# First feed-forward: weight quarters in the order dense, dense, modulation, modulation

## Chip, cores and metric

The kernel runs on one core of one Trainium2 chip. The metric is the device time of one execution in microseconds (us), the median of the runs made.

## What is computed

One inference step of a two-layer encoder over 384 token rows: 256 of a prompt (one stream) and 16 for each of 8 running streams. Width is 2048, feed-forward width 5632. Each layer has a token mixer (layer 0 attention, layer 1 causal pooling) and a SwiGLU feed-forward, and each of these four sub-layers is modulated by vectors that depend on the stream alone:

```
mod = silu(c) @ w_ada + b_ada              # nine streams, 2048 x 12288 weights in each layer
h   = rms_norm(x, g_ffn) * (1 + scale2) + shift2
x   = x + gate2 * ((silu(h @ w_gate) * (h @ w_up)) @ w_down)
```

Everything is float32. Weights are read from HBM once.

## The kernel before, in words

**Units.** Weights come in units of 1 MB: 512 rows by 512 columns, as 4 row tiles of 128 rows. There are four slots for units. `raw[:, s]` is the buffer that a DMA fills, and `w_hi`/`w_lo` share their bytes with `w_top`/`w_mid`. Unit `n` of weight group `W` is in slot `n % 4` (`unit`, "quarter" in the change's name).

**Dense units** (`w_gate`, `w_up`, `w_down`). ScalarE copies `raw` to the rounded `w_hi` (L569), and VectorE computes `w_lo = raw - w_hi` (L956). TensorE then takes three matmuls for each pair of tiles (`product`: L1511, L1512, L1513), 128x128 weights against 384 tokens, 48 matmuls a unit.

**Modulation units** (`w_ada`). ScalarE copies `raw` to bf16 `w_top` (L576), and VectorE makes two more bf16 pieces in two instructions (`mid`, L961 and L963). TensorE takes 12 bf16 matmuls of 512 columns (`ada_sub`, L1538), each with a stationary operand only 32 columns wide, so that four of them stand side by side in the array (`q = C32 * (i % 4)`). Four modulation units make one block of 512 modulation values. ScalarE then copies the block out (`mod_out`, L596), TensorE transposes it (`ada_turn`, four matmuls at L1547), and VectorE sums it into `modT` (`mod_in`, L986 and L989).

**One chunk of the first feed-forward** (`mixed_chunk`, 11 chunks in a hardware loop on TensorE, of which the first 10 are a loop on ScalarE and VectorE). A chunk is 512 of the 5632 hidden features and takes 20 units: 0 to 7 the gate's four dense units in turn with the four modulation units of block `a`, 8 to 15 the same for up and block `a + 1`, and 16 to 19 the four dense units of the down product. The gate accumulates in banks 4 to 7, up in banks 0 to 3. Block `a` accumulates in bank 3, block `a + 1` in bank 7.

**What sets the order.** Each engine's order is written out by hand and engines meet through counting semaphores. SP loads the units in their order, a slot's next unit as soon as VectorE has read `raw` (`load` waits for `lo_ready`). ScalarE converts unit `n + 4` only once TensorE has used unit `n` (`free` waits for `sub_used`). VectorE follows ScalarE (`hi_ready`), and TensorE waits for `lo_ready` at a dense unit and for `top_rest` at a modulation unit. Between weights, ScalarE applies Silu to the gate (`gate_out`, L851) and rounds the product (`acts_hi`, L846), VectorE multiplies gate by up (`times_up`, L1378) and adds the down product into the residual `x` (`down_add`, L1065, L1072, L1075), and GpSimd makes `act_lo` (L539).

**Before the first chunk** the residual is normalised (`norm_apply(1, W_FFN0)`). VectorE scales four groups of feature tiles (`norm_scale`, L1030 and following), ScalarE shifts and rounds them into `h_hi` (L643, L647), and VectorE writes `h_lo` (`norm_split`, L1042). Units 2 and 3 of the first chunk are converted in between (`BETWEEN`), 0 and 1 earlier, in the last block of the attention's output product. TensorE starts unit 0 when the first half of group 0 is there, and needs group `j` for the gate's `j`-th dense unit.

Of the kernel before, what the change touches and what calls it, by code (L numbers as in the profile page):

```python
# [25 lines left out]
ds = bass.ds  # L26
# [26 lines left out]
W_FFN0 = W_O + 8  # L53
# [48 lines left out]
def encoder_step(nc, x_prompt, x_sample, c_prompt, c_sample, cache_k, cache_v, state_pool,  # L102
# [5 lines left out]
    with ctx:  # L108
# [24 lines left out]
        h_hi, H0 = nxt("h_hi", [P, KT, TOK], f32r)  # L133
# [115 lines left out]
        def rows(w):  # L249

            return w.rearrange("(k p) n -> p k n", p=P)
# [35 lines left out]
        def unit(W, n):  # L287

            return W + n // 4, n % 4

        def y_bank(q):
            return down_bank(q)

# [33 lines left out]
        def _(sp):  # L327
            def load(W, s, src):
                sp.wait_ge(lo_ready, 4 * W + s - 3)
                sp.dma_start(raw[:, s], src).then_inc(raw_loaded[s], 16)  # L330
# [26 lines left out]
            def load_pair(W, j, dense, layer, a):  # L357

                for n, src in ((2 * j, dense), (2 * j + 1, ada_src(layer, a, j))):
                    load(*unit(W, n), src)  # L360

            def qkv_rows(n, j):

# [82 lines left out]
            def load_mixed(W, c, layer, a):  # L446

                for i, w in enumerate((w_gate, w_up)):
                    for j in range(4):
                        load_pair(W + 2 * i, j, rows(w[0, j * 512:(j + 1) * 512, ds(c * 512, 512)]), layer, a + i)  # L450
                load_down(W + 4, 0, c)

            load_mixed(W_FFN0, 0, 0, ADA_FFN)
# [101 lines left out]
        def _(act):  # L555
# [21 lines left out]

            def mixed(W, n):

                W, s = unit(W, n)  # L580
                if n % 2:
                    top(W, [s])
                else:
                    hi(W, [s])

            def dense(W, n):

                W, s = unit(W, n)
                hi(W, [s])

            def mod_out(used, a, acc_bank, done=sub_used):

                act.wait_ge(done, used)
                if not isinstance(a, int) or a:
                    act.wait_ge(ada_t, a)
                act.activation(mod[:], bank[:, acc_bank, :], ACT.Copy).then_inc(mod_ready, 1)  # L596
# [251 lines left out]
            def gate_out(used):  # L848

                act.wait_ge(sub_used, used)  # L850
                act.activation(act_f[:], bank[:, 4:8, 0:TOK], ACT.Silu).then_inc(gate_taken, 1)  # L851

            def mixed_chunk(W, c, a, following, last=False):

                for n in range(4, 10):
                    mixed(W, n)
                gate_out(4 * W + 7)
                mixed(W, 10); mod_out(4 * W + 8, a, 3); mixed(W, 11)
                for n in range(12, 16):
                    mixed(W, n)  # L860
                dense(W, 16); dense(W, 17)
                for m in range(4):
                    acts_hi(c, m)
                mod_out(4 * W + 16, a + 1, 7)
                dense(W, 18); dense(W, 19)
                for s in range(4):
                    following(W, 20 + s)
                    if last and s < 3:
                        square(2, s)
                    elif last:  # L870
                        square_last(2)
# [75 lines left out]
        def _(dve):  # L947
# [16 lines left out]

            def mixed(W, n):

                W, s = unit(W, n)
                if n % 2:
                    mid(W, s)
                else:  # L970
                    lo(W, [s])

            def dense(W, n):

                W, s = unit(W, n)
                lo(W, [s])
# [68 lines left out]
            def norm_apply(n, W):  # L1045

                norm_scale(n, 0, 2, 1)
                norm_scale(n, 2, 2, 2)
                norm_split(n, 0, 2, 1, half_ready)
                norm_split(n, 2, 2, 2)  # L1050
                for g in range(1, 4):
                    if g >= 2:
                        dve.wait_ge(h_ready, HR[n] + g - 1)
                    norm_scale(n, 4 * g, 4, g + 2)
                    for s in BETWEEN[n][g]:
                        (mixed if n == 1 else dense)(W, s)
                    if g >= 2:
                        norm_split(n, 4 * g - 4, 4, g + 1)
                norm_split(n, 12, 4, 5)

# [309 lines left out]
            def times_up(c, used):  # L1370

                dve.wait_ge(gate_taken, c + 1)
                for m in range(4):
                    if m < 3:
                        dve.wait_ge(up_tile, 3 * c + m + 1)
                    else:
                        dve.wait_ge(sub_used, used)
                    dve.tensor_tensor(act_f[:, m], act_f[:, m], bank[:, m, 0:TOK], ALU.mult).then_inc(act_f_ready, 1)  # L1378
# [7 lines left out]
            def mixed_chunk(W, c, a, layer, r, following, last=False):  # L1386

                for n in range(4, 12):
                    mixed(W, n)
                mod_in(a, 4)  # L1390
                for n in range(12, 16):
                    mixed(W, n)
                dense(W, 16); dense(W, 17)
                times_up(c, 4 * W + 15)
                dense(W, 18)
                mod_in(a + 1, 3)
                dense(W, 19)
                dve.wait_ge(ada_done, a + 2)
                for s in range(4):
                    down_add(4 * W + 17 + s, s, r, layer, last and s == 3)  # L1400
                    if not last or s < 3:
                        following(W, 20 + s)
                    if last and s < 3:
                        square_sum(2, s)
# [103 lines left out]
        def _(pe):  # L1508
# [18 lines left out]
            def ada_sub(W, n, a, j, acc_bank):  # L1527

                W, s = unit(W, n)
                if j == 0:  # L1530
                    pe.wait_ge(mod_ready, a)
                pe.wait_ge(top_rest, 4 * (a - ADA_QKV) + j + 1)
                for k in range(4):
                    kt = 4 * j + k
                    for piece, w in enumerate((w_top[:, s, 0, k], mid_top(s)[:, k], w_top[:, s, 1, k])):
                        i = 3 * kt + piece
                        q = C32 * (i % 4)
                        last = pe.matmul(bank[q:q + C32, acc_bank, :], c32[:, kt], w, start=(i < 4), stop=(i >= 3 * KT - 4))  # L1538
                last.then_inc(sub_used, 1)

            def ada_turn(a, t_bank):

# [304 lines left out]
            def mixed_chunk(W, c, a, r, hr):  # L1847

                pe.wait_ge(residual_taken, r - 1)
                for j in range(4):  # L1850
                    if j:
                        pe.wait_ge(h_ready, hr + j + 1)
                    else:
                        pe.wait_ge(half_ready, 1)
                    to_features(W, 2 * j, 4, h_hi, h_lo, 4 * j, j == 0, j == 3, second_half=None if j else hr + 1)
                    if j == 0:
                        pe.wait_ge(residual_taken, r)
                    ada_sub(W, 2 * j + 1, a, j, 3)
                for m in range(4):
                    if m == 3:  # L1860
                        pe.wait_ge(mod_ready, a + 1)
                    last = tile_features(W, 8, m, 0, h_hi, h_lo, 0, True, False)
                last.then_inc(sub_used, 1)
                pe.wait_ge(gate_taken, c + 1)
                ada_turn(a, 4)
                ada_sub(W, 9, a + 1, 0, 7)
                for j in (1, 2):
                    to_features(W, 8 + 2 * j, 0, h_hi, h_lo, 4 * j, False, False)
                    ada_sub(W, 9 + 2 * j, a + 1, j, 7)
                up_tail(W, 14)  # L1870
                ada_sub(W, 15, a + 1, 3, 7)

                w, s = unit(W, 16)
                pe.wait_ge(lo_ready, 4 * w + s + 1)
                pe.wait_ge(ada_done, a + 1)
                for k in range(4):
                    pe.wait_ge(act_ready, 4 * c + k + 1)
                    for m in range(3):
                        cols = slice(m * P, (m + 1) * P)
                        product(bank[:, 4 + m, 0:TOK], w_hi[:, s, k, cols], w_lo[:, s, k, cols],  # L1880
                                act_hi[:, k, :], act_lo[:, k, :], k == 0, k == 3)
                ada_turn(a + 1, 3)
                last = tile_features(W, 16, 3, 4, act_hi, act_lo, 0, True, True)
                last.then_inc(sub_used, 1)
                pe.wait_ge(ada_done, a + 2)
                down_rest(W, 16, r)
# [104 lines left out]
```

## Time and profile before

| | |
|---|---|
| median of 3 runs | 3416.63 us |
| lowest and highest | 3412.81 and 3418.68 us |
| span of the profiled execution, first to last instruction | 3414.0 us |
| mean granted TensorE clock (1 is 2.4 GHz) | 0.985 |
| TensorE matmul busy | 3265.0 us, 96% |
| VectorE busy | 2119.0 us, 62% |
| ScalarE busy | 1309.1 us, 38% |
| GpSimd busy | 137.6 us, 4% |
| DMA | 646.49 MB, mean 189 GB/s |

The profiled execution is given by its span; a time of its own outside the span is not listed. Its span is 2.6 us under the median of the runs. Busy time alone doesn't say what an engine's work costs: TensorE's matmuls overlap, each row lasting longer than the distance to the next, so distances between starts are what counts. A timeline line reads: start in us, duration in us, engine, line of the kernel, operation, output and inputs, count, and in brackets how long the engine had been idle and what released it.

### The profile page before, as it was taken

The numbers are of one execution on the slowest core, as the hardware profiler recorded it, in microseconds if no ns is written. First come the engines' busy times: TensorE is split into PE (matmuls) and PEld (weight loads), VectorE is DVE, ScalarE is ACT, GpSimd is POOL, SyncE is SP. The second block draws the span as 40 slices with busy tenths as digits, with TensorE's granted clock in tenths as the row PEclk, the third lists the DMA queues.
The fourth block names the chain that finished last, engine by engine and source line by source line (L and its number), as shares of the span: only waits on it lengthen the run. The fifth ranks groups of instructions, "written<-read, shape, count | busy, mean of one in ns | idle before, by whom it ended". The sixth has DMA issues, their size and how long they took to land.

```text
span 3414.0 us, 47966 instructions
## 1 busy us (share of the span) xinstructions
PE 3265.0 (96%) x20219; PEld 2953.3 (87%) x20219; DVE 2119.0 (62%) x1855; ACT 1309.1 (38%) x994; POOL 137.6 (4%) x124
## 2 busy tenths in 40 slices
PE   7999998889989999999999999769999999999999
PEld 3677776667979999999999999659999999999999
DVE  4488885567887777777776777784344443344443
ACT  3344444455453343334433443443223222322221
POOL 0000000000000000000000000110000000000000
PEclk9999999999999999999999999889999999999999
DMA  9777777877645555556555565544343333333331
GB/s 352 269 263 248 249 244 251 304 278 263 231 160 185 199 206 185 193 176 210 205 177 192 184 209 197 190 158 145 123 131 127 123 124 133 125 123 124 127 130 62
DMA packets 325816, 646.49 MB, mean 189 GB/s; under 512 B 10881, under 2 KB 13513, under 8 KB 325321
## 3 DMA queue, kind: packets, MB, share of 16 engines
q1 hardware_dynamic: 317144, 630.17, 54.1%
q10 hardware_dynamic: 8586, 15.09, 1.3%
q8 instruction: 65, 1.06, 0.1%
q14 instruction: 21, 0.17, 0.0%
HBM read 631.46 MB, written 14.74 MB: 189 GB/s over the span
## 4 chain that ended last, share of the span: by engine, by line
PE 88%; DVE 5%; DMA 4%; ACT 2%; issue 1%; POOL 0%; SPq 0%; ACTq 0%; DVEq 0%; POOLq 0%
PE bank L1511 23%; PE bank L1513 23%; PE bank L1512 23%; PE bank L1595 3%; PE bank L1538 3%; PE bank L1597 3%; PE bank L1596 3%; DMA raw<-in_w_ada 2%; PE bank L1701 1%; DMA raw<-in_cache_v 1%; PE bank L1523 1%; PE bank L1742 1%; DVE w_lo L956 0%; PE bank L1547 0%; DMA early_raw<-in_w_qkv 0%
## 5 line engine op out<-in xcount | busy, mean ns | idle before, releaser
L956 DVE TENSOR_TENSOR w_lo<-raw,w_hi 128x2048 fp32r<-128x2048 f32 x323 | 738.9, 2290 | 877.7 <-ACT w_hi L569 877.7
L569 ACT ACTIVATE w_hi<-raw 128x2048 fp32r<-128x2048 f32 x323 | 616.3, 1915 | 1352.4 <-PE bank L1513 1168.7
L1511 PE MATMUL bank<-h_hi,w_hi 128*128 128x384 f32 x3136 | 1063.9, 339 | 34.3 <-DVE h_lo L1042 24.1
L1512 PE MATMUL bank<-h_lo,w_hi 128*128 128x384 f32 x3136 | 1052.2, 336 | 0.0
L1513 PE MATMUL bank<-h_hi,w_lo 128*128 128x384 f32 x3120 | 1047.7, 336 | 0.0
L1511 PEld LDWEIGHTS bank<-h_hi,w_hi 128*128 128x128 f32 x3136 | 591.9, 189 | 79.3 <-issue 67.1
L1512 PEld LDWEIGHTS bank<-h_lo,w_hi 128*128 128x128 f32 x3136 | 592.3, 189 | 0.0
L1513 PEld LDWEIGHTS bank<-h_hi,w_lo 128*128 128x128 f32 x3120 | 589.0, 189 | 0.0
L1511 PE MATMUL bank<-act_hi,w_hi 128*128 128x384 f32 x1408 | 472.9, 336 | 0.0
L1513 PE MATMUL bank<-act_hi,w_lo 128*128 128x384 f32 x1408 | 470.6, 334 | 0.0
L1512 PE MATMUL bank<-act_lo,w_hi 128*128 128x384 f32 x1408 | 470.5, 334 | 0.0
L961 DVE TENSOR_TENSOR w_mid<-raw,w_top 128x2048 f32<-128x2048 f32 x144 | 329.1, 2285 | 14.7 <-ACT w_top L576 14.7
L576 ACT ACTIVATE w_top<-raw 128x2048 bf16<-128x2048 f32 x144 | 273.7, 1901 | 161.7 <-PE bank L1513 128.5
L963 DVE TENSOR_TENSOR w_top<-w_mid 128x2048 bf16<-128x2048 f32 x144 | 330.0, 2292 | 5.0
L1511 PEld LDWEIGHTS bank<-act_hi,w_hi 128*128 128x128 f32 x1408 | 264.3, 188 | 4.8 <-POOL act_lo L539 4.8
L1512 PEld LDWEIGHTS bank<-act_lo,w_hi 128*128 128x128 f32 x1408 | 264.4, 188 | 0.0
L1513 PEld LDWEIGHTS bank<-act_hi,w_lo 128*128 128x128 f32 x1408 | 264.3, 188 | 0.0
L1595 PE MATMUL bank<-w_hi,h_hi 128*128 128x512 f32 x480 | 192.4, 401 | 2.6 <-DVE w_lo L956 2.6
L539 POOL TENSOR_TENSOR act_lo<-act_f,act_hi 128x384 fp32r<-128x384 f32 x88 | 87.9, 1015 | 2652.0 <-ACT act_hi L846 2650.7
L1597 PE MATMUL bank<-w_hi,h_lo 128*128 128x512 f32 x480 | 187.7, 391 | 0.0
L1596 PE MATMUL bank<-w_lo,h_hi 128*128 128x512 f32 x480 | 187.4, 390 | 0.0
L1072 DVE SCALAR_TENSOR_TENSOR x<-bank,modT,x 128x256 f32<-128x256 f32 x384 | 158.6, 475 | 0.0
(231 smaller groups left out, 2501.5 us busy)
## 6 DMA issues: line engine op xcount, KB each, us to landing
raw<-in_w_ada SPq DMA_DIRECT2D x192, 1024.0 KB, 5.8
raw<-in_w_gate SPq DMA_DIRECT2D x88, 1024.0 KB, 5.2
raw<-in_w_up SPq DMA_DIRECT2D x88, 1024.0 KB, 5.2
raw<-in_w_down SPq DMA_DIRECT2D x88, 1024.0 KB, 5.1
raw<-in_w_qkv SPq DMA_DIRECT2D x40, 1024.0 KB, 5.2
raw<-in_cache_k SPq DMA_DIRECT2D x32, 1024.0 KB, 6.0
raw<-in_cache_v SPq DMA_DIRECT2D x32, 1024.0 KB, 7.2
raw<-in_w_o SPq DMA_DIRECT2D x15, 1024.0 KB, 5.1
```

Source lines behind the costliest of these rows:

```text
L569: act.activation(w_hi[:, s], raw[:, s], ACT.Copy).then_inc(hi_ready, 1)
L576: act.activation(w_top[:, s, 0], raw[:, s], ACT.Copy).then_inc(hi_ready, 1)
L956: dve.tensor_tensor(w_lo[:, s], raw[:, s], w_hi[:, s].bitcast(f32), ALU.subtract).then_inc(lo_ready, 1)
L961: dve.tensor_tensor(w_mid[:, s], raw[:, s], w_top[:, s, 0], ALU.subtract).then_inc(lo_ready, 1)
L963: dve.tensor_tensor(w_top[:, s, 1], w_mid[:, s], mid_top(s), ALU.subtract).then_inc(top_rest, 1)
L1072: step.mark(dve.scalar_tensor_tensor(xv, ps[:, k, 0:PROMPT], mod[:, k, 0:1], xv, ALU.mult, ALU.add))
L1511: pe.matmul(out, w, a, start=start, stop=False)
L1512: pe.matmul(out, w, al, start=False, stop=False)
L1513: return pe.matmul(out, wl, a, start=False, stop=stop)
L1595: pe.matmul(out, h_hi[:, kt, cols], w_hi[:, s, k], start=(kt == 0), stop=False)
L1596: pe.matmul(out, h_hi[:, kt, cols], w_lo[:, s, k], start=False, stop=False)
L1597: last = pe.matmul(out, h_lo[:, kt, cols], w_hi[:, s, k], start=False, stop=(kt == KT - 1))
```

## The change

In the first feed-forward alone, the units of each group of four go dense, dense, modulation, modulation (before: dense, modulation, dense, modulation). SP loads them in that order (`load_four`), and ScalarE and VectorE choose the conversion by `in_ffn`. TensorE takes two dense units and then the two modulation units behind one another (`ada_two`). ScalarE's Silu moves with the gate's end, from behind unit 6 to behind unit 5. The second down unit (17) now takes the slot of the last up unit (13), so ScalarE converts it behind `acts_hi`, and VectorE multiplies gate by up ahead of the split of unit 17. In the normalisation ahead of the first chunk VectorE writes `h_lo` of group `g - 1` ahead of converting the weight unit.

```diff
+        def in_ffn(W, n):
+            return not isinstance(W, int) or W + n // 4 >= W_FFN0
...
+            def load_four(W, f, dense, layer, a):
+
+                for i in range(2):
+                    load(*unit(W, 4 * f + i), dense(2 * f + i))
+                for i in range(2):
+                    load(*unit(W, 4 * f + 2 + i), ada_src(layer, a, 2 * f + i))
...
-                    for j in range(4):
-                        load_pair(W + 2 * i, j, rows(w[0, j * 512:(j + 1) * 512, ds(c * 512, 512)]), layer, a + i)
+                    for f in range(2):
+                        load_four(W + 2 * i, f, lambda j: rows(w[0, j * 512:(j + 1) * 512, ds(c * 512, 512)]), layer, a + i)
...
             def mixed(W, n):
+                rest = n % 4 >= 2 if in_ffn(W, n) else n % 2
                 W, s = unit(W, n)
-                if n % 2:
+                if rest:
...
             def mixed_chunk(...):
-                for n in range(4, 10):
+                for n in range(4, 9):
                     mixed(W, n)
-                gate_out(4 * W + 7)
-                mixed(W, 10); mod_out(4 * W + 8, a, 3); mixed(W, 11)
+                gate_out(4 * W + 6)
+                mixed(W, 9); mod_out(4 * W + 8, a, 3); mixed(W, 10); mixed(W, 11)
                 for n in range(12, 16):
                     mixed(W, n)
-                dense(W, 16); dense(W, 17)
+                dense(W, 16)
                 for m in range(4):
                     acts_hi(c, m)
                 mod_out(4 * W + 16, a + 1, 7)
-                dense(W, 18); dense(W, 19)
+                dense(W, 17); dense(W, 18); dense(W, 19)
...
                     norm_scale(n, 4 * g, 4, g + 2)
+                    if n == 1 and g >= 2:
+                        norm_split(n, 4 * g - 4, 4, g + 1)
                     for s in BETWEEN[n][g]:
                         (mixed if n == 1 else dense)(W, s)
-                    if g >= 2:
+                    if n != 1 and g >= 2:
                         norm_split(n, 4 * g - 4, 4, g + 1)
...
-                dense(W, 16); dense(W, 17)
-                times_up(c, 4 * W + 15)
-                dense(W, 18)
+                dense(W, 16)
+                times_up(c, 4 * W + 14)
+                dense(W, 17); dense(W, 18)
...
+            def ada_two(W, f, a, acc_bank):
+
+                for i in range(2):
+                    ada_sub(W, 4 * f + 2 + i, a, 2 * f + i, acc_bank)
...
-                    to_features(W, 2 * j, 4, h_hi, h_lo, 4 * j, j == 0, j == 3, second_half=None if j else hr + 1)
-                    if j == 0:
+                    to_features(W, j + j // 2 * 2, 4, h_hi, h_lo, 4 * j, j == 0, j == 3, second_half=None if j else hr + 1)
+                    if j == 1:
                         pe.wait_ge(residual_taken, r)
-                    ada_sub(W, 2 * j + 1, a, j, 3)
+                    if j % 2:
+                        ada_two(W, j // 2, a, 3)
...
-                ada_sub(W, 9, a + 1, 0, 7)
-                for j in (1, 2):
-                    to_features(W, 8 + 2 * j, 0, h_hi, h_lo, 4 * j, False, False)
-                    ada_sub(W, 9 + 2 * j, a + 1, j, 7)
-                up_tail(W, 14)
-                ada_sub(W, 15, a + 1, 3, 7)
+                to_features(W, 9, 0, h_hi, h_lo, 4, False, False)
+                ada_two(W + 2, 0, a + 1, 7)
+                to_features(W, 12, 0, h_hi, h_lo, 8, False, False)
+                up_tail(W, 13)
+                ada_two(W + 2, 1, a + 1, 7)
```

## Rows read from the trace of the kernel before

**Rows 1.** The page: the chain that ended last, by engine.

```profile
PE 88%; DVE 5%; DMA 4%; ACT 2%; issue 1%; POOL 0%; SPq 0%; ACTq 0%; DVEq 0%; POOLq 0%
```

**Rows 2.** Stretches: two whole chunks; us, engines' busy us (count), PEclk, DMA share, GB/s.

```profile
1014.20:1123.03 108.83, 108.83 (x684) 102.48 (x688) 78.34 (x60) 44.15 (x29) 3.97 (x4) 1.00 0.57 195
...
1340.66:1449.47 108.81, 108.81 (x684) 102.46 (x684) 78.34 (x60) 44.15 (x29) 3.97 (x4) 1.00 0.57 193
```

**Rows 3.** Timeline, ScalarE: Silu; conversions started by TensorE freeing a slot.

```profile
1340.66 1.45 ACT L851 ACTIVATE act_f<-bank 128x1536 f32<-128x1536 f32 x1 [4.31 <-PE bank L1513]
...
1388.21 1.92 ACT L569 ACTIVATE w_hi<-raw 128x2048 fp32r<-128x2048 f32 x1 [4.59 <-PE bank L1513]
1396.53 1.91 ACT L576 ACTIVATE w_top<-raw 128x2048 bf16<-128x2048 f32 x1 [6.40 <-PE bank L1513]
...
1421.49 1.91 ACT L569 ACTIVATE w_hi<-raw 128x2048 fp32r<-128x2048 f32 x1 [5.05 <-PE bank L1513]
...
1430.82 1.91 ACT L569 ACTIVATE w_hi<-raw 128x2048 fp32r<-128x2048 f32 x1 [5.61 <-PE bank L1513]
```

**Rows 4.** Timeline, TensorE: one modulation unit between two dense ones.

```profile
1340.28 0.34 PE L1513 MATMUL bank<-h_hi,w_lo 128*128 128x384 f32 x1
1340.55 0.39 PE L1538 MATMUL bank<-w_top,c 128*32 128x512 bf16 x1
...
1340.78 0.39 PE L1538 MATMUL bank<-w_mid,c 128*32 128x512 bf16 x1
...
1341.00 0.41 PE L1538 MATMUL bank<-w_mid,c 128*32 128x512 bf16 x1
...
1341.62 0.33 PE L1512 MATMUL bank<-h_lo,w_hi 128*128 128x384 f32 x1
```

**Rows 5.** Timeline, TensorE: transposes of a modulation block inside a dense unit.

```profile
1385.28 0.34 PE L1513 MATMUL bank<-act_hi,w_lo 128*128 128x384 f32 x1
1385.46 0.60 PE L1547 MATMUL bank<-ident,mod 128*128 128x128 f32 x4
...
1386.07 0.34 PE L1512 MATMUL bank<-act_lo,w_hi 128*128 128x384 f32 x1
```

**Rows 6.** Timeline, TensorE in the attention: a long run of 32-column matmuls.

```profile
784.75 2.69 PE L1742 MATMUL bank<-raw,zs_past 128*32 128x128 f32 x92
```

**Rows 7.** Timeline, VectorE behind the Silu: units 10 and 11, then unit 12.

```profile
1343.95 2.29 DVE L956 TENSOR_TENSOR w_lo<-raw,w_hi 128x2048 fp32r<-128x2048 f32 x1 [3.85 <-ACT w_hi L569]
1346.23 2.29 DVE L961 TENSOR_TENSOR w_mid<-raw,w_top 128x2048 f32<-128x2048 f32 x1
1348.56 2.29 DVE L963 TENSOR_TENSOR w_top<-w_mid 128x2048 bf16<-128x2048 f32 x1
1350.76 0.60 DVE L986 TENSOR_REDUCE modT<-bank 128x432 f32 x1
...
1351.93 2.29 DVE L956 TENSOR_TENSOR w_lo<-raw,w_hi 128x2048 fp32r<-128x2048 f32 x1 [0.23 <-ACT w_hi L569]
```

**Rows 8.** The page: DMA issues, KB each, us from issue to landing.

```profile
raw<-in_w_ada SPq DMA_DIRECT2D x192, 1024.0 KB, 5.8
```

**Rows 9.** Timeline, VectorE around the first chunk: units 2, 3, `h_lo` of group 1, unit 4.

```profile
973.60 2.29 DVE L956 TENSOR_TENSOR w_lo<-raw,w_hi 128x2048 fp32r<-128x2048 f32 x1
...
978.92 2.28 DVE L961 TENSOR_TENSOR w_mid<-raw,w_top 128x2048 f32<-128x2048 f32 x1
...
983.45 1.75 DVE L1042 TENSOR_TENSOR h_lo<-nbuf,h_hi 128x1536 fp32r<-128x1536 f32 x1
...
993.89 2.29 DVE L956 TENSOR_TENSOR w_lo<-raw,w_hi 128x2048 fp32r<-128x2048 f32 x1 [1.47 <-ACT w_hi L569]
```

**Rows 10.** Timeline, TensorE in the first chunk: starts of units 2 and 4.

```profile
985.33 0.55 PE L1511 MATMUL bank<-h_hi,w_hi 128*128 128x384 f32 x1 [3.80 <-DVE h_lo L1042]
...
996.23 0.44 PE L1511 MATMUL bank<-h_hi,w_hi 128*128 128x384 f32 x1
```

**Rows 11.** Stretch, TensorE, unit 2 of the first chunk: us, busy us (count), PEclk, DMA share, GB/s.

```profile
985.33:995.40 10.07, 10.07 (x48) 0.83 0.03 11
```

More of the change, by code:

```diff
@@ L965, in mixed @@
             def mixed(W, n):
+                rest = n % 4 >= 2 if in_ffn(W, n) else n % 2
                 W, s = unit(W, n)
-                if n % 2:
+                if rest:
                     mid(W, s)
```

## The prediction

> **What bounds the kernel now.** I read the page's chain first: TensorE holds 88% of it [rows 1]. Then one chunk of the first feed-forward, cut from Silu to Silu: 108.8 us, in which TensorE is busy from end to end at the full clock (2.4 GHz), VectorE for 78.3 and ScalarE for 44.2 [rows 2]. So in this stage nothing but TensorE's own spacing counts, and the other engines and the DMAs only have to stay in time. Last the timelines, for that spacing. ScalarE's conversions there start when TensorE frees a slot, so the distance of two of them is what TensorE took for what lies between: 8.32 us for one dense unit of the down product, 9.33 for a dense unit and a modulation unit [rows 3]. A modulation unit thus costs 1.01 us. Its 12 matmuls account for less: they go four at a time, and the three waves start 0.225 apart, which is 0.675 in all [rows 4]. The rest is at the two changes of form. From the last dense matmul to the first wave it is 0.27 where dense matmuls are 8.32/48 = 0.173 apart, and from the last wave to the second dense matmul it is 0.62 where 0.225 + 0.173 would do. That is 0.10 and 0.22, together 0.32; as 1.01 - 0.675 it comes to 0.33 [rows 3, 4]. **A pair of changes of form costs 0.33 us**, and a chunk has eight pairs.
>
> A check: 12 dense units at 8.32, 8 modulation units at 1.01 and two transposes. A set of transposes takes 1386.07 - 1385.46 - 0.173 = 0.44 inside a dense unit [rows 5]. The sum is 99.8 + 8.1 + 0.9 = 108.8, which is the chunk [rows 2].
>
> **The change, part by part.** *The order of units on TensorE.* Each chunk then has four runs of two modulation units where it had eight of one. Matmuls, loads and bytes are the same, and four pairs of changes go: 4 x 0.33 = 1.3 us a chunk. No row shows two modulation units in a row, so I bound a merge. At the least it gives nothing, if the second unit starts as expensively as after a dense one; a loss is excluded, since no change of form is added. At the most it gives 0.33, since the columns still have to pass. I take 0.33, because of the nearest row: 92 matmuls with the same 32-column form follow one another in 2.69 us, 27 to 29 ns each, across the waits and counts between groups of 16 [rows 6]. Nothing is paid there at a boundary, and the pace is twice the 0.225/4 = 56 ns wanted here.
>
> The first of the two transposes now sits between two dense units, not ahead of a modulation unit. I cost that at nothing: the second sits between dense matmuls already, and the sum above closes with the same 0.44 for both.
>
> *What must stay in time in a chunk.* VectorE has the tight spot behind the Silu, where unit 9's split is followed by four instructions for units 10 and 11 back to back, by the sums of the block (`mod_in`), and only then by unit 12's split. Measured from the Silu's start: unit 9's split starts at 3.3, as unit 10's does now, and two modulation splits take 4 instructions of 2.2 to 2.3, to 14.6. The sums take 1351.93 - 1350.76 = 1.2 with a short idle time in it, and the split of unit 12 takes 2.2, so it is there at 18.0 [rows 7]. TensorE then wants unit 12 after two modulation units, unit 8, a set of transposes, unit 9 and two more modulation units: 2 x (2 x 0.675 + 0.33) + 2 x 8.32 + 0.44 = 20.4. **Slack 2.4 us.** Unit 10 itself is wanted at 18.7 and there at 10.1; unit 11 is there at 14.6. A unit's raw slot is refilled 5.8 us after its issue [rows 8], and the load of unit 12 is issued when unit 8's split ends, ahead of the Silu. The queue of SP meets the same 20 loads and waits as before, and what stands behind a waiting load is a unit wanted later.
>
> *Gate times up ahead of unit 17's split.* Unit 17 now uses the slot of unit 13, which ends the up product. From that end, E, TensorE takes two modulation units and unit 16 with its transposes: 1.7 + 8.3 + 0.4 = 10.4. ScalarE waits for the two (1.7), copies the block out (not rowed; allowed as long as a conversion, 1.9), converts 17 (1.9) and VectorE splits it (2.3): E + 7.8 at the latest [rows 3, 7]. Slack 2.6 us, so nothing is paid. Were the split left ahead, ScalarE and VectorE would wait for each other, since `acts_hi` now stands ahead of unit 17. The multiplication itself gains nothing: unit 16 was waiting for neither. The activations even get 0.675 more, since two modulation units now stand between up's end and unit 16. The Silu moves with the gate's end, and bank 3 is copied out ahead of unit 8's fourth tile, 6 us on. The adds into `x` keep their places between the down units; bank 3 is wanted one dense unit later than before.
>
> *The first chunk pays.* Unit 2 becomes a modulation unit, so VectorE has two instructions for it where it had one: 983.45 - 978.92 = 4.53 against 2.29, so 2.2 to 2.3 more, between 973.60 and unit 4's split at 993.89 [rows 9]. TensorE starts unit 4 when that split is done (993.89 + 2.29 = 996.18, start 996.23) [rows 9, 10]. Everything between is one chain, VectorE's norm of group 3, ScalarE's rounding and conversion of unit 4, so unit 4 starts **2.3 us later**, near 998.5. The new place of `norm_split` helps what isn't last: unit 1's features come at 973.60 + 4.53 + 3.1 + 1.8 = 983.0, against 985.3 for unit 2 before (3.1 is what lies between 973.60 + 2.2 and 978.92) [rows 9, 10]. Unit 1 and two modulation units are over by 983.1 + 10.1 + 1.7 = 994.9 at the latest, so TensorE then stands idle for at least 3.6 us ahead of unit 4. Before, a gap of 3.8 stood ahead of unit 2, and that unit ran at a mean clock of 0.83, starting at the lower level (1.2 GHz): 10.07 us, not 8.32 [rows 10, 11]. I expect the same for unit 4, **1.7 us more**. Bounds: 0, if the clock holds, and 3.4, if the lower level lasts twice as long as in that unit. The first of this chunk's merges falls ahead of unit 4's wait and gives nothing; three are left. The last attention block has one VectorE instruction less (unit 1 is dense now), ahead of a wait for TensorE: nothing.
>
> *The last chunk* converts pool weights behind its down units as before, and the rest of the kernel starts earlier by the sum.
>
> **The sum.** Ten chunks with 4 merges and one with 3: 43 x 0.33 = 14.2 us less. First chunk 2.3 + 1.7 = 4.0 us more. Together 10.2 less: 3414.0 to 3403.8 for the span, and from the median, which stands 2.6 above the span, 3416.6 to **3406.4 us**, 0.30% less. About 0.2% (6.8 us) is what a measurement of this kernel tells from no change.
>
> **Rivals.** *(A) Merges give little.* A run of 24 small matmuls outlasts what TensorE's queue has read ahead during a dense unit, and from there goes at the pace of issue. Within a unit all 12 keep 56 ns [rows 4], which a short head start could cover; against it speak the 92 matmuls at under 30 ns [rows 6]. At no gain at all the first chunk's 4.0 stays: 3420.6. At half: 3416.6 + 4.0 - 7.1 = 3413.5. Both count as no change. The Trainium skill, in "TensorE: Matmul & The Clock Gate", section "Wait — 56ns, not 53.3ns?", has a rule on this side: where decoding in hardware is off, the sequencer needs about 62 ns for each matmul, and that binds when the array's work is shorter. By it a second unit would take 12 x 62 = 0.74 us, and and 43 merges would give an estimated 43 x 0.26 = 11.2 us, 3409.4; the row of 92 disagrees with it.
>
> *(B) VectorE falls behind unit 12: slower.* Two modulation splits behind one another leave 2.4 us. If the queue from unit 9 to unit 12 comes late by more than that, through a late load or slower instructions, TensorE stands in each of 10 or 11 chunks. It decides from 2.4 + 1.3 = 3.7 us late in each chunk, where the gain is gone. At 5 late it costs 2.6 x 11 = 29 against 10.2 gained: 3435. Against it: the chunks repeat to 0.02 us [rows 2], and VectorE's instructions to 0.1 [rows 7].
>
> *(C) The first chunk costs more*, as unit 4's wait pushes units 5 to 7 too. Their splits follow 2 to 3 us behind each other and have 8 us each, so I give it 2 us at most: 3408.4. It is part of the forecast's range.
>
> **How the numbers follow.** Forecast with (C) 0.78, its range 3402 to 3411: the merge 0.30 to 0.36 (1.3 us each way), the clock 0 to 3.4 (1.7 each way), (C) +2, and runs that differ by a few us. (A) 0.16, (B) 0.06. The limit for faster is 3409.8, and of the forecast's 0.78 some 0.08 lies above it. Faster 0.70, same 0.24 (0.16 + 0.08), slower 0.06. The range is 3401 to 3414: the forecast's, one more us below for the runs, and (A) down to half of the gain.
>
> **What would show it.** Right: chunks of 107.5 us from Silu to Silu, with TensorE busy throughout; in a merged run six waves 0.225 apart and one gap of 0.27 ahead; unit 12's split some 2.4 ahead of its matmuls; unit 4 of the first chunk starting near 998.5 and running at a mean clock near 0.83. Wrong: a gap between the third and fourth waves or a pace over 0.225 (A), TensorE waiting for L956 at unit 12 or 17 (B), or a first chunk over 4 us later at its second Silu than units and merges make it (C).

## The result and the profile after

The changed kernel takes 3403.8 us (median of 5 runs, 3402.8 to 3406.0); the kernel before 3414.8 (median of 5: the three runs above and two more). The ratio is 0.9965, 95% interval 0.9953 to 0.9977: faster by 0.35%, a small effect whose interval leaves out 1. In later runs, again with the kernel before beside it, the ratio was 0.9965 once more (0.9954 to 0.9977). The forecast was 3406.4, between 3401 and 3414.

The profiled execution has a span of 3401.1 us. Two whole chunks, cut from Silu to Silu, in the stretches of the changed kernel (engines' busy us and counts, PEclk, DMA share, GB/s):

```profile
1014.59:1122.07 107.48, 107.48 (x684) 102.98 (x684) 78.13 (x60) 44.29 (x29) 3.93 (x4) 1.00 0.57 191
1337.03:1444.51 107.48, 107.48 (x684) 102.98 (x684) 78.11 (x60) 44.28 (x29) 3.92 (x4) 1.00 0.58 195
```

A chunk lasts 107.48 us where it lasted 108.81 to 108.83 [rows 2], with the same 684 matmuls, TensorE still busy from end to end and the other engines' work unchanged. That is 1.33 less, ten times from the first Silu to the eleventh. Where it comes from is seen in the timeline of TensorE, at the two modulation units behind the gate of the first chunk:

```profile
1014.22 0.34 PE L1527 MATMUL bank<-h_hi,w_lo 128*128 128x384 f32 x1
1014.48 0.39 PE L1552 MATMUL bank<-w_top,c 128*32 128x512 bf16 x1
...
1014.71 0.39 PE L1552 MATMUL bank<-w_mid,c 128*32 128x512 bf16 x1
...
1014.93 0.41 PE L1552 MATMUL bank<-w_mid,c 128*32 128x512 bf16 x1
...
1015.16 0.39 PE L1552 MATMUL bank<-w_mid,c 128*32 128x512 bf16 x1
...
1015.37 0.41 PE L1552 MATMUL bank<-w_mid,c 128*32 128x512 bf16 x2
...
1015.61 0.40 PE L1552 MATMUL bank<-w_mid,c 128*32 128x512 bf16 x1
...
1016.21 0.33 PE L1526 MATMUL bank<-h_lo,w_hi 128*128 128x384 f32 x1
```

Six waves (four matmuls each), 0.21 to 0.24 apart, and nothing between the third and the fourth, where the second unit begins. The gap ahead (0.26) and the slow return behind (0.60 from the last wave to the second dense matmul) are those of a single unit [rows 4], and are paid once for two.

The first chunk has grown. TensorE's timeline there, with the starts of units 0, 1 and 4, and ahead of them the start of unit 0 in the kernel before:

```profile
969.54 0.68 PE L1511 MATMUL bank<-h_hi,w_hi 128*128 128x384 f32 x1 [8.56 <-DVE h_lo L1042]
```

```profile
966.99 0.68 PE L1525 MATMUL bank<-h_hi,w_hi 128*128 128x384 f32 x1 [8.56 <-DVE h_lo L1054]
980.59 0.44 PE L1525 MATMUL bank<-h_hi,w_hi 128*128 128x384 f32 x1 [2.54 <-DVE h_lo L1054]
...
995.88 0.69 PE L1525 MATMUL bank<-h_hi,w_hi 128*128 128x384 f32 x1 [5.25 <-DVE w_lo L967]
```

And the stretches of unit 1 (all engines, as above) and of unit 4 (TensorE alone: busy us, count, PEclk, DMA share, GB/s):

```profile
980.59:989.00 8.41, 8.41 (x48) 8.27 (x48) 8.31 (x6) 2.65 (x6) 0.00 (x0) 1.00 0.39 125
```

```profile
995.88:1006.00 10.12, 10.12 (x48) 0.81 0.89 308
```

Unit 4 starts 28.9 us after unit 0, where it was 26.7 (996.23 [rows 10] less 969.54). It was released by its own split, and it runs at a mean clock of 0.81, starting at 1.2 GHz. Unit 1, behind a gap of 2.5 us, ran at the full clock.

Single executions differ ahead of all this. Unit 0 started at 967.0 here and at 969.5 before, and between 967 and 977 in the runs below, in stages that the change leaves as they were but for one VectorE instruction less in the last attention block. So the trace is compared from unit 0's start on, to the first Silu of the second feed-forward (before, then after):

```profile
2336.07 1.46 ACT L851 ACTIVATE act_f<-bank 128x1536 f32<-128x1536 f32 x1 [5.10 <-PE bank L1513]
```

```profile
2323.14 1.46 ACT L862 ACTIVATE act_f<-bank 128x1536 f32<-128x1536 f32 x1 [5.10 <-PE bank L1527]
```

That is 1366.5 us before (2336.07 - 969.54) and 1356.2 after (2323.14 - 966.99): **10.4 us less**, where the sum said 10.2. It is made of 13.3 less between the first and the eleventh Silu and 2.9 more ahead of the first; behind the eleventh Silu the two take 233.7 and 233.8.

### The profile page after: what moved, and what is told of

It is laid out like the page before. It is cut to its first block, busy times and chain, and to the rows that moved or that the text cites. A ratio compares the mean times of both kernels' runs of the same rounds, so it can differ in the third digit from the quotient of the medians.

```text
span 3401.1 us, 47966 instructions
## 1 busy us (share of the span) xinstructions
PE 3250.1 (96%) x20219; PEld 2957.6 (87%) x20219; DVE 2116.7 (62%) x1855; ACT 1310.5 (39%) x994; POOL 137.1 (4%) x124
## 4 chain that ended last, share of the span: by engine, by line
PE 87%; DVE 5%; DMA 4%; ACT 2%; issue 1%; POOL 0%; SPq 0%; ACTq 0%; DVEq 0%; POOLq 0%
PE bank L1525 23%; PE bank L1527 23%; PE bank L1526 23%; PE bank L1614 3%; PE bank L1616 3%; PE bank L1615 3%; PE bank L1552 3%; DMA raw<-in_w_ada 3%; PE bank L1720 1%; DMA raw<-in_cache_v 1%; PE bank L1537 1%; DMA raw<-in_cache_k 0%; DVE w_lo L967 0%; PE bank L1566 0%; DMA early_raw<-in_w_qkv 0%
```

## The experiments

Theory: TensorE bounds the stage, each merge of two modulation units saves one pair of changes of form, 0.33 us, and the first chunk pays some 4 us because VectorE is late for unit 4 and the clock has fallen by then. Rivals: the gain comes from another part of the change; the second modulation unit is slowed by issue; VectorE's queue has less room than worked out. Ratios are to the kernel before on the same chip. "First Silu" is its start after the start of unit 0, which is 44.7 before (1014.22 - 969.54) and 47.6 after (1014.59 - 966.99).

**The new order in the up half alone.** The gate half, its loads, the Silu's place and the norm are as before.

```diff
-                rest = n % 4 >= 2 if in_ffn(W, n) else n % 2
+                rest = n % 4 >= 2 if in_ffn(W, n) and 8 <= n < 16 and not (isinstance(W, int) and W < W_FFN0) else n % 2
...
-                    to_features(W, j + j // 2 * 2, 4, h_hi, h_lo, 4 * j, j == 0, j == 3, second_half=None if j else hr + 1)
-                    if j == 1:
+                    to_features(W, 2 * j, 4, h_hi, h_lo, 4 * j, j == 0, j == 3, second_half=None if j else hr + 1)
+                    if j == 0:
                         pe.wait_ge(residual_taken, r)
-                    if j % 2:
-                        ada_two(W, j // 2, a, 3)
+                    ada_sub(W, 2 * j + 1, a, j, 3)
```

> The new order in the up half alone (units 8 to 15); the gate half keeps dense, modulation, dense, modulation, and the norm ahead of the first chunk keeps its old order. If each merge of two modulation units is worth 0.33 us and nothing else counts, a chunk lasts 108.81 - 2 x 0.33 = 108.15 us from Silu to Silu, the first chunk is as in the kernel before (first Silu 44.7 us after unit 0's start), and 22 merges give 7.3 us: ratio 0.998. If the gain comes from elsewhere (the Silu's new place, the slots of the down units), the chunk is not halfway but at 107.5 or at 108.8.

Ratio 0.9982 (0.9972 to 0.9991). First Silu at 44.65. The stretch of its first whole chunk:

```profile
1015.80:1123.95 108.15, 108.15 (x684) 102.68 (x684) 78.13 (x60) 44.28 (x29) 3.93 (x4) 1.00 0.59 196
```

108.15, halfway to the hundredth: the gain goes with the number of merges. The Silu's place and the gate's slots, which are the old ones here, have no share in it; neither has unit 17's new place, which is in this kernel and adds nothing to the two merges.

**The first chunk's gate half in the old order**, all else changed. The first chunk is taken out of the loops of TensorE, ScalarE and VectorE.

```diff
-            return not isinstance(W, int) or W + n // 4 >= W_FFN0
+            return not isinstance(W, int) or W + n // 4 >= W_FFN0 + 2
...
+            mixed_chunk(W_FFN0, 0, ADA_FFN, R_FFN0, 4, first=True)
-            with pe.Fori(0, CHUNKS) as c:
+            with pe.Fori(1, CHUNKS) as c:
...
+                    if first:
+                        ada_sub(W, 2 * j + 1, a, j, 3)
+                    elif j % 2:
+                        ada_two(W, j // 2, a, 3)
```

> The changed kernel, with the first chunk's gate half and the norm in the old order. If the first chunk pays what the trace says (unit 8 stands 3.6 us later after unit 0's start than before, 49.3 against 45.7), that comes back: first Silu 44.7 us after unit 0's start, chunks of 107.48, and 3.6 us less than the changed kernel: ratio to the kernel before 0.996. If the first chunk's cost is only moved elsewhere, the total stays that of the changed kernel (0.9965).

Ratio 0.9962 (0.9947 to 0.9977), median 3401.2. First Silu at 45.5 (1022.22 - 976.76), 0.8 later than expected, with unit 2 at a mean clock of 0.76 instead of 0.83 [rows 11]. Chunks of 107.44. From unit 0 to the first Silu of the second feed-forward: 1354.5 (2331.23 - 976.76), 1.7 less than the changed kernel, not 3.6. Of the missing 1.9 us, 0.8 is the first Silu. The rest lies behind the eleventh Silu, where this execution took 235.2 to the next feed-forward (2331.23 - 2095.99) and the changed kernel's 233.8. Why that stretch varies stays open; it was 230.6 to 235.2 in all kernels here but the one with unit 17 split ahead. Up to the eleventh Silu 3.2 of the 3.6 us do come back (1119.2 from unit 0's start against 1122.4). The total can't tell it.

**`norm_split` back behind the weight unit** in the norm ahead of the first chunk.

```diff
-                    if n == 1 and g >= 2:
-                        norm_split(n, 4 * g - 4, 4, g + 1)
                     for s in BETWEEN[n][g]:
                         (mixed if n == 1 else dense)(W, s)
-                    if n != 1 and g >= 2:
+                    if g >= 2:
                         norm_split(n, 4 * g - 4, 4, g + 1)
```

> The changed kernel with the write of h_lo of the group before put back behind the conversion of the weight unit. Theory (the clock decides): unit 1 starts 4.5 us later, 18.1 after unit 0's start, after a long gap and so at the lower clock, and ends at 28.1; with two modulation units unit 4 starts at 29.8 instead of 28.9, but without a gap and so at the full clock: the first Silu comes 46.7 after unit 0's start, 0.9 us earlier than in the changed kernel (47.6). Rival (the move was needed): unit 4 is late and at the lower clock too, first Silu at 48.4.

First Silu at 46.8 (1014.80 - 968.03), against 46.7 expected. A single run, 3403.1 us. The stretch of unit 1, then that of unit 4 (TensorE alone):

```profile
986.16:996.20 10.04, 10.04 (x48) 0.81 0.02 9
...
998.00:1006.50 8.50, 8.50 (x50) 1.00 0.92 308
```

Unit 1 is 4.5 us later, behind a gap of 7.35, and is the one that runs at the lower clock. Unit 4 then follows without a gap, at the full clock. The move of `norm_split` that the change brought makes unit 1 early and TensorE idle later on, and costs 0.8 us net. One execution shows it; five with the move (and no matmuls of no use) had their first Silu at 47.4 to 48.6, all later than here.

**Unit 17 split ahead of gate times up**, as before the change, on both engines.

```diff
-                dense(W, 16)
+                dense(W, 16); dense(W, 17)
                 for m in range(4):
                     acts_hi(c, m)
                 mod_out(4 * W + 16, a + 1, 7)
-                dense(W, 17); dense(W, 18); dense(W, 19)
+                dense(W, 18); dense(W, 19)
...
-                dense(W, 16)
+                dense(W, 16); dense(W, 17)
                 times_up(c, 4 * W + 14)
-                dense(W, 17); dense(W, 18)
+                dense(W, 18)
```

> The changed kernel with unit 17 converted and split ahead of gate times up again, on ScalarE and on VectorE. From the end E of up's last unit: conversion of 17 to E + 1.9, its split to E + 4.2, four products of 0.5, rounding and GpSimd 1.6 behind the first: the first activation tile is there at E + 6.3, where TensorE wants it at E + 1.7. Theory (the second part of the change is needed): TensorE stands 4.6 us in each chunk, so 112.1 us from Silu to Silu, and up to 1.7 more if the clock falls; in all 51 to 70 us over the changed kernel. Rival (it is hidden): 107.5.

A single run, 3481.0 us. Stretches of two chunks, and what TensorE's weight load (PEld) waited for in the second (us in all, times, longest):

```profile
1131.06:1246.20 115.14, 110.16 (x684) 105.59 (x684) 78.23 (x60) 44.20 (x29) 3.89 (x4) 0.97 0.55 182
1246.20:1360.21 114.01, 109.03 (x684) 104.46 (x684) 78.24 (x60) 44.20 (x29) 3.90 (x4) 0.99 0.56 184
```

```profile
PEld bank L1525 <- POOL act_lo L549: 5.5, 1, 5.5
```

TensorE stands 4.98 us in each chunk (115.14 - 110.16), for the first of the four `act_lo` tiles that GpSimd makes, where 4.6 was expected. It is also busy 1.5 to 2.7 us longer for the same matmuls, at a mean clock of 0.97 to 0.99: the clock falls behind the gap. The mean of nine chunks is 114.4 us ((2046.49 - 1016.61) / 9), 7.0 over the changed kernel's. In all it is 77 us over the changed kernel (3481.0 - 3403.8), more than the 51 to 70 expected, since both the gap and the clock cost more than allowed for. So the second part of the change is what the first part needs: without it the kernel is 65 us slower than the kernel before beside it (3415.8).

**One, then two more instructions on VectorE** ahead of units 10, 11 and 12 in each chunk.

```diff
                 for n in range(4, 12):
+                    if n == 9:
+                        w, s = unit(W, n)
+                        dve.wait_ge(hi_ready, 4 * w + s + 1)
+                        for _ in range(1):
+                            step.mark(dve.tensor_tensor(w_lo[:, s], raw[:, s], w_hi[:, s].bitcast(f32), ALU.subtract))
+                            own()
                     mixed(W, n)
```

> The changed kernel with one more VectorE instruction of 2.2 us in each chunk (the split of unit 9 is written twice), ahead of units 10, 11 and 12. In the changed kernel unit 12's split ends 17.8 us after the Silu's start and TensorE wants it at 20.4, by the sums of the rows: slack 2.5. One more instruction must cost nothing: 107.5 us from Silu to Silu. If the slack is less than the rows say, the chunk is longer by the missing part.

107.48 us from Silu to Silu (1123.14 to 1230.62), 3404.6 us in a single run. In the changed kernel unit 12's split is VectorE's:

```profile
1352.54 2.29 DVE L967 TENSOR_TENSOR w_lo<-raw,w_hi 128x2048 fp32r<-128x2048 f32 x1
```

It starts 15.5 behind the Silu at 1337.03 and ends at 17.8. Here it starts at 17.7 (1355.85 - 1338.11). It costs nothing in a chunk.

> The same with two more instructions, 4.5 us: 2.0 over the slack, so 109.5 us from Silu to Silu and TensorE waiting for w_lo at unit 12, some 22 us in all. If VectorE's queue had more room than worked out, 107.5.

With `range(2)`: 3439.2 us in a single run. Six of ten chunks take 109.77 us, where 109.5 was expected, but four take 111.3. From unit 0 to the second feed-forward it is 29.8 us more than in the changed kernel (1386.0 against 1356.2), where some 22 was expected. Two chunks, then a stretch of 4 us inside the first of them, right behind its gap; and a wait of this kind in another chunk (us in all, times, longest):

```profile
1132.30:1243.60 111.30, 109.23 (x684) 0.98 0.56 188
1353.40:1463.17 109.77, 107.70 (x684) 1.00 0.57 191
...
1154.00:1158.00 4.00, 3.29 (x14) 0.76 0.43 132
```

```profile
PE bank L1531 <- DVE w_lo L967: 2.1, 1, 2.1
```

Both chunks have the same gap of 2.07 us (111.30 - 109.23, 109.77 - 107.70), so the slack was 4.5 - 2.1 = 2.4 us. In the first the clock fell behind it and took 1.5 us more.

**Matmuls of no use in the first chunk's gap.** TensorE's first chunk stands outside the loop; the results go to a bank that the up product overwrites.

```diff
                         ada_two(W, j // 2, a, 3)
+                    if first and j == 1:
+                        for i in range(26):
+                            pe.matmul(bank[:, 1, 0:TOK], h_hi[:, i % 8, 0:P], h_hi[:, i % 8, :], start=True, stop=True)
```

> The changed kernel with 26 matmuls of no use (the result is overwritten) behind the first two modulation units of the first chunk, some 4.5 us, in the gap of 5.3 us that stands ahead of unit 4. If the lower clock in unit 4 comes from that gap, unit 4 runs at the full clock and the first Silu comes 45.9 us after unit 0's start, 1.7 less than 47.6. If something else slows unit 4 (its operands, the engines beside it), it stays at 47.6.

First Silu at 46.7 (1020.20 - 973.50), 0.8 later than expected. The stretches of unit 1 and unit 4:

```profile
987.17:997.20 10.03, 10.03 (x48) 0.83 0.33 105
1003.30:1011.70 8.40, 8.40 (x51) 1.00 0.96 337
```

Unit 4 did run at the full clock, beside the same engines and on the same operands: the gap is the cause. But in this execution the lower clock fell into unit 1, behind a gap of 3.2, so the matmuls of no use began 1.6 later than planned for, and the last of them pushed unit 4 back from 28.9 to 29.8.

**Another order of VectorE's norm**, alone:

```diff
+                    norm_scale(n, 4, 4, 3)
+                    dve.wait_ge(h_ready, HR[n] + 1)
+                    norm_scale(n, 8, 4, 4)
+                    norm_split(n, 4, 4, 3)
+                    mixed(W, 2)
+                    dve.wait_ge(h_ready, HR[n] + 2)
+                    norm_scale(n, 12, 4, 5)
+                    mixed(W, 3)
+                    norm_split(n, 8, 4, 4)
+                    norm_split(n, 12, 4, 5)
```

> The changed kernel with VectorE's work ahead of the first chunk in another order: norm of groups 1 and 2, h_lo of group 1, unit 2, norm of group 3, unit 3, h_lo of groups 2 and 3, unit 4. If VectorE's row of instructions sets unit 4's start, with idle time in it that the order can take out, unit 4 starts 26.9 us after unit 0, not 28.9, still at the lower clock: first Silu at 45.6. If ScalarE or a DMA sets it, it stays near 47.6.

TensorE's timeline: unit 0, the first matmul of a modulation unit that had to wait (unit 3), unit 4.

```profile
972.07 0.68 PE L1537 MATMUL bank<-h_hi,w_hi 128*128 128x384 f32 x1 [8.57 <-DVE h_lo L1054]
993.22 0.39 PE L1564 MATMUL bank<-w_top,c 128*32 128x512 bf16 x1 [0.98 <-DVE w_top L974]
...
998.76 0.69 PE L1537 MATMUL bank<-h_hi,w_hi 128*128 128x384 f32 x1 [4.69 <-DVE w_lo L967]
```

Unit 4 starts at 26.7, 2.2 earlier, so VectorE's row of instructions does set it. In the changed kernel VectorE stood idle for 2.0 us in that row, waiting for ScalarE (0.55 and 1.46); the new order takes this out. The first Silu came at 46.4, not 45.6: unit 4 ran at a mean clock of 0.70 this time. A single run, 3407.9 us.

**Both together**, with 22 matmuls of no use, and the changed kernel itself once more beside it:

> VectorE's order of the run before (norm of group 2 and h_lo of group 1 ahead of unit 2) together with 22 matmuls of no use, some 3.8 us, behind the first chunk's first two modulation units. Theory: unit 4 starts 26.7 us after unit 0 and, with no long gap ahead, stays at the full clock, so the first Silu comes 43.4 after unit 0's start, 4.2 less than in the changed kernel; chunks 107.48; some 4 us less than the changed kernel in all, ratio to the kernel before 0.9955. Rival (the first chunk's loss is made up later or falls elsewhere): same total as the changed kernel.

> The changed kernel as it is, beside the run above and the kernel before on one chip. By both theories the ratio of its first measurement, 0.9965; by the trace 10.4 us less than before from unit 0 on, so 0.997.

Unit 4 starts at 26.9 (1000.52 - 973.58), behind a gap of 0.74. Its first matmul, and its stretch (TensorE alone):

```profile
1000.52 0.41 PE L1537 MATMUL bank<-h_hi,w_hi 128*128 128x384 f32 x1 [0.74 <-DVE w_lo L967]
...
1000.50:1008.80 8.30, 8.28 (x48) 1.00 0.88 301
```

First Silu at 43.9 (1017.44 - 973.58), 3.9 earlier than in the changed kernel beside it (1016.36 - 968.57 = 47.8) and 0.8 earlier than in the kernel before; 43.4 was expected. At the eleventh Silu the lead is still 3.9 (1118.7 from unit 0's start against 1122.6), so it isn't given back in the feed-forward. The changed kernel takes 1356.6 from unit 0 to the second feed-forward here (2325.13 - 968.57), against 1356.2 the first time. In the total it can't be told: 3404.0 against 3404.8, ratios 0.9962 (0.9949 to 0.9976) and 0.9965 (0.9954 to 0.9977).

## Why the prediction was right

**The bound and the price of a merge: right.** The sum took 0.33 us from the distance of conversions less the waves. Measured: 1.33 a chunk for four merges, 0.67 for two in the kernel with the up half alone (108.82 - 108.15). The bound from both sides was put at its upper end by the row of 92 narrow matmuls [rows 6], a row of another form (fp32, 128 columns), and the runs bear that choice out. The Trainium skill says in "TensorEngine Tiling (Array Packing)", section "Key Properties", that a change of the tiling mode, not of the tile, drains TensorE; the waves agree, 0.26 ahead of a run and nothing inside it.

**Rival (A), issue: refuted.** The fourth to sixth waves keep the pace of the first three, 56 ns a matmul. The rule in the Trainium skill's "TensorE: Matmul & The Clock Gate", section "Wait — 56ns, not 53.3ns?", that puts the sequencer at about 62 ns for each matmul where decoding in hardware is off does not bind here, over 24 matmuls; with which way of decoding the kernel ran, no run shows.

**Rival (B), VectorE behind the Silu: did not come, and its place was right.** The working gave unit 12's split at 18.0 and a slack of 2.4. The trace has 17.8, and the first matmul of unit 12 at 20.1 (1357.16 - 1337.03). One more instruction of 2.2 costs nothing, two of together 4.5 cost a gap of 2.07. The price of the rival was too low: the prediction charged only the wait, and in some chunks the clock fell too (111.3, not 109.8).

**Rival (C): did not come.** From unit 4's start to the first Silu TensorE has no gap, and the first chunk's distance from Silu to Silu is the 107.48 of the others.

**Gate times up: right that it costs nothing**, and that it is needed. The reason given was that the two engines would otherwise wait for each other. By the code that holds only if VectorE alone keeps the old order, which no run tried. With both in the old order the kernel runs, and pays 7.0 us a chunk.

**The first chunk: right in size.** Unit 4 was 2.2 later (2.3 forecast). The clock's term was 1.7: from unit 4's start to the Silu it is 18.7, where the runs that kept the full clock took 16.9 (1017.44 - 1000.52), so 1.8 here, and 2.8 in the run with the new norm order (1018.49 - 998.76 less 16.9). Taken to the start of unit 8, the chunk is 3.6 us longer than before: the first Silu is 2.9 later (47.6 - 44.7), and 1.7 of modulation units follow it instead of 1.0. The forecast had 4.0 less one merge, 3.7. The prediction gave the gap ahead of unit 4 as at least 3.6, with unit 1 at the lower clock; unit 1 ran at the full clock, and the gap was 5.25. That the clock then cost 1.8, so near the 1.7, is in part luck: in the six executions in which unit 4 ran slow it cost 1.6 to 2.8.

**What the prediction credited wrongly** is the move of `norm_split`. It said that this helps what isn't last, and had unit 1's start right (13.5 after unit 0's; 13.6 measured). But the move does harm: TensorE gets unit 1 early and then stands so long that the unit that counts starts at the lower clock. Undone, the first Silu is 0.8 earlier, in the one execution that there is.

**The total.** 10.2 less was forecast, and 10.4 is what the trace shows from unit 0 on. The medians differ by 11.0 (3414.8 - 3403.8), and the forecast's 3406.4 was counted from a median of three runs that stood at 3416.6. With five it is 3414.8, from which the same sum gives 3404.6.

## What to carry to other kernels

Where an engine is busy from end to end, look at the distances between starts at each change of instruction form, and price a change as what two neighbours take together less what each takes in its own run. Then group like with like, and check how far the engine that feeds them falls behind, by adding instructions to it until the stage grows. At the start of a stage it can be worth less than nothing to make the first unit early, if the engine then waits ahead of the one that counts.

## What was not expected of the hardware

A gap of 2.07 us, the same in each chunk, was followed by the lower clock in some chunks and not in others of one execution (111.3 and 109.8 us). In the first chunk gaps of 2.5 us (changed kernel) left the full clock; 3.2 us (the run with matmuls of no use) did not, nor did gaps of 3.1 to 3.7 in two more executions (the runs with one more instruction and with unit 17 split ahead), where both unit 1 and unit 4 ran slow and the first Silu came at 48.3 and 48.6. What a fall costs varied too, from 1.5 us to 2.8. A sum for such a stage should carry 0 to 3 us for each gap of this size, not one value.
